# A streaming encoder step on one core: smaller bias write, one mask product a bank, state products and norm moved

## The chip, the core and the metric

The kernel runs on one core of one Trainium2 chip. It uses all engines of that core: TensorE (PE in the rows) for matrix products and transposes into the eight banks of PSUM, VectorE (DVE), ScalarE (ACT), GpSimd (POOL), and the transfer queues that SP, ACT and POOL issue. The metric is device time of one execution in microseconds. The kernel before took 1349.67 us, the median of three runs (1347.54 to 1352.28).

## What is computed

One step of a one-layer encoder over 384 tokens in three tiles of 128: tile 2 is the next 16 frames of eight running streams (the "sample"), tiles 0 and 1 are the 256 frames of a new prompt. Everything is 32-bit float. In short:

```
xn  = rmsnorm(x, g_mix)
q,k,v,o,i,f | aq,ak,av,iq,ik,iw = split(xn @ w_in)
h_m = mLSTM over 4 heads of 128 (with state C, n, m per stream), then headnorm * g_hn * sigmoid(o)
h_a = attention, 8 heads of 64, over the top-k keys that an indexer picks, plus a relative-position bias
h   = x + concat(h_m, h_a) @ w_out
hn  = rmsnorm(h, g_ffn)
s   = (hn @ w_pq) . subkeys            # 8 heads x 2 halves x 128 subkeys
top 16 of each half -> 256 sums -> top 16 -> 16 experts a head, gates = softmax(top 16)
a   = gelu(hn . U[expert])             # 128 experts a token, from a table of 16384
y   = rmsnorm(h + sum(gates * a * V[expert]), g_fin)
```

Outputs are y, the new keys, values and indexer keys, and the new mLSTM states.

## The kernel before

There is one program per engine, written out by hand, with semaphores between them. Two orders rule all. The first is PSUM: a written-out plan (`psum_plan`, L63, and `unit_banks`, L106) names every use of a bank in order; use n takes bank n mod 6, TensorE begins it (`begin`, L878) only when use n - 6 has been read, and either VectorE or ScalarE is its reader. Banks 6 and 7 hold long sums. The second is each engine's own instruction order: a waiting instruction holds all behind it.

**Preparation, streams first.** SP (L409 on) loads inputs and weight chunks of 2 MB into a ring of three (`load_ring`), a step ahead of use. TensorE makes the sample's features chunk by chunk (`sample_features`, L905, and `by_token`, L912). The relative-position bias is one product of a 32-row table (`bvec`, 8 heads x 511 distances, L950). SP writes it to a DRAM scratch once for each of 128 rows (L442), so that a skewed read of the scratch gives every query row its own shift; eight small copies (L448) read the sample's bias back, and LP[0] and LP[1], the prompt's biases, are read by one transfer each (L480, L495). The indexer's scores (L923, name `ri`) lead to the top 36 keys and a mask `negS` of 0 or -1e30 for each token row (L1493). The masked logits `lg` (L986 to L989) are three banks of three, three and two streams; for each stream one product of a 128x128 table `spread` with `negS` adds the mask (L921), then four products of 32 rows add the logits (L923). The spread table is loaded by SP (L445) behind the bias write and the load of the states `CT` (L443).

Then come softmax, attention, mLSTM numerators (L1046), head norm and the output projection of the sample into banks 6 and 7 (L1060 for the attention half, L1069 for the mLSTM half). VectorE adds x (L1611), sums squares (L1399), ScalarE takes the root (L622), VectorE scales by 1/root and g_ffn into `hn` (L1606), TensorE turns `hn` (L1087), ScalarE copies it out (`turned`, L671), and the first query `qs0` starts (`sample_query`, L1101). POOL multiplies the new states' weighted values (L562) and decays the states (L566); `new_state` adds TensorE's product on VectorE (L1622). Scores (L1113) go to VectorE, which picks subkeys and experts (`route_subkeys`, `route_pairs`, `route_experts`, L1632 to L1692). When the first 16 experts a token are known, POOL starts to gather (L580).

**The expert loop.** For each of the three tiles (order 2, 0, 1), 128 gathers bring one expert row pair (U and V, 8 KB) for each of the 128 tokens, 1 MB in all, into one of eight slots. A unit is two experts. VectorE forms the dots (`dots`, L1707), ScalarE gelu, gate and a diagonal (L698 to L707), TensorE adds diag x V to banks 6 and 7 by four matmul records an expert (`weigh`, L1134); a slot is free when that is done. In the first tile every fourth expert (e % 4 == 3) is weighed on VectorE instead (L1717). Into the 64 units of the first tile the whole prompt work is laid, a step a unit (`first_tile`, one function for each engine: L722, L1215, L1780): queries, states, indexer, attention, mLSTM, output projection (L1192), norm, prompt queries (L1145), with weight chunks in two buffers of 2 MB (`load_late`). The later tiles have routing only.

The lines that set what the change touches:

```
L59    return n == 0 and e % 4 == 3                                   # on_vector
L442   sp.dma_start(d["scratch"][:, :, 0:511], over(bvec, 1, P)).then_inc(bvec_out, 16)
L921   mm(o, spread[:, s, :], negS, start=True, stop=False, skip_group_check=True)
L1571  link(v.tensor_tensor(st[:, c:c + 2], st[:, c:c + 2], cols[:, 1, t, 2 * i:2 * i + 2], ALU.max))
L1606  v.scalar_tensor_tensor(hn[t], xr[:, t, :], st[:, lo + 8:lo + 9], gffn, ALU.mult, ALU.mult).then_inc(hn_ok, 1)
L1116  new_state(0); turn_hn(SAMPLE, 1); sample_query(0); new_state(1); scores(0); sample_query(1)   # TensorE, waits left out
L1694  new_state(0); new_state(1); route_subkeys(0, 0); route_pairs(0, 0); route_experts(0)          # VectorE
```

## Time and profile before

| | before |
|---|---|
| median of the runs, us | 1349.67 |
| the profiled execution: its own time / its span, us | 1350.36 / 1348.20 |
| busy: PE, DVE, ACT, POOL, us | 1076.6, 838.3, 391.8, 436.1 |
| mean granted PE clock | 0.937 |
| moved by the transfers | 484.22 MB, 359 GB/s over the span |
| of that, the gathers | 402.68 MB |
| first gather issued; first dots of tile 1; of tile 2, us | 209.9; 670.6; 1024.7 |

The span runs from the first to the last instruction; the execution's own time has 2.16 us around it. Busy shares are means over parts with different limits, so the table is to be read with the windows by stage below. A matmul in 32-bit float is two records in the trace, and their ends are modelled. The granted clock is a share of 2.4 GHz; it has two levels, 1.0 and 0.5.

### The profile page before, as it was taken

The page shows a single profiled execution, that of the slowest core. Times are in us where ns is not written, and L with a number is a line of the kernel's source. Part 1 is how long each engine was busy: PE and PEld are TensorE (multiplying, and loading weights), DVE is VectorE, ACT ScalarE, POOL GpSimd, SP SyncE. Part 2 cuts the span into 40 slices and gives each one's busy share as a digit, 9 for nine tenths or more (in the row PEclk, how much of TensorE's full clock was granted, in tenths as well). Part 3 has the DMA queues.
Part 4 walks back from the last instruction along what each step waited for, and adds up shares of the span by engine and source line. Part 5 has one row for each costly group of instructions (what it writes and reads, how often), then busy time and mean ns, then how long its engine had stood idle before and what let it go on. Part 6 is the DMA issues. An engine that isn't in the chain of part 4 may idle for free.

```text
span 1348.2 us, 11119 instructions
## 1 busy us (share of the span) xinstructions
PE 1076.6 (80%) x3592; PEld 582.9 (43%) x3592; DVE 838.3 (62%) x1949; ACT 391.8 (29%) x1175; POOL 436.1 (32%) x406
## 2 busy tenths in 40 slices
PE   6829975889989999978799877777676777777776
PEld 5719554655635744435465433323222222222222
DVE  3402236769997576766868799996445545454444
ACT  0202002223344344233423333333223222222222
POOL 1000133323332333323333444344343333343431
PEclk9958977989999999989899989889998999999999
DMA  9767409999999989998989999999999999999996
GB/s 359 204 173 272 189 0 375 423 419 363 401 397 367 370 355 423 348 367 339 389 331 344 336 367 395 395 394 409 421 422 381 424 421 421 422 421 422 421 422 264
DMA packets 72520, 484.22 MB, mean 359 GB/s; under 512 B 7464, under 2 KB 17292, under 8 KB 19216
## 3 DMA queue, kind: packets, MB, share of 16 engines
q0 software_dynamic: 55296, 402.68, 74.0%
q1 hardware_dynamic: 16336, 80.08, 16.1%
q10 hardware_dynamic: 832, 0.77, 0.2%
q8 instruction: 28, 0.46, 0.1%
q14 instruction: 28, 0.23, 0.0%
HBM read 475.79 MB, written 7.71 MB: 359 GB/s over the span
## 4 chain that ended last, share of the span: by engine, by line
PE 39%; DMA 27%; DVE 27%; ACT 4%; issue 2%; POOL 0%; DVEq 0%; ACTq 0%; POOLq 0%
DMA arena<-in_peer_uv,arena 23%; PE ps L1134 18%; DVE arena L1707 11%; PE ps L1145 5%; PE ps L912 4%; DMA arena<-in_spreads 3%; PE ps L905 3%; PE ps L1192 2%; ACT arena L701 1%; DVE arena L1635 1%; DVE arena L1642 1%; ACT arena L707 1%; DVE arena L1636 1%; DVE arena L1684 1%; DVE arena L1682 1%
## 5 line engine op out<-in xcount | busy, mean ns | idle before, releaser
L1134 PE MATMUL ps<-arena 128*128 128x512 f32 x1408 | 677.1, 626 | 209.9 <-ACT arena L707 208.3
L580 POOL DMA_INDIRECT arena<-in_peer_uv,arena x384 | 412.3, 1074 | 708.4 <-PE ps L1134 629.4
L1707 DVE CUSTOM_DVE_ANT_0 arena<-arena 128x1024 f32<-128x1024 f32 x380 | 456.5, 1224 | 233.7 <-DMA arena<-in_peer_uv,arena 230.8
L1134 PEld LDWEIGHTS ps<-arena 128*128 128x128 f32 x1408 | 267.4, 198 | 577.4 <-issue 289.5
L698 ACT ACTIVATE arena<-arena 128x2 f32<-128x2 f32 (+1 forms) x194 | 39.4, 203 | 601.4 <-DVE arena L1707 591.9
L1145 PE MATMUL ps<-arena 128*128 128x256 f32 x576 | 131.4, 381 | 0.7 <-ACT arena L607 0.7
L707 ACT ACTIVATE arena<-arena 128x128 f32<-128x128 f32 x352 | 124.0, 395 | 6.3
L1145 PEld LDWEIGHTS ps<-arena 128*128 128x128 f32 x576 | 110.3, 192 | 31.7 <-issue 17.3
L607 ACT ACTIVATE arena<-ps 128x256 f32<-128x256 f32 (+2 forms) x85 | 39.2, 479 | 253.9 <-PE ps L1145 85.3
L701 ACT ACTIVATE arena<-arena 128x1 f32<-128x1 f32 x384 | 92.3, 287 | 6.4
L912 PE MATMUL ps<-arena 128*128 128x512 f32 x144 | 66.0, 613 | 0.0
L562 POOL TENSOR_TENSOR arena<-arena 128x1032 f32<-128x1032 f32 x4 | 8.7, 2178 | 130.9 <-PE ps L1046 107.6
L912 PEld LDWEIGHTS ps<-arena 128*128 128x128 f32 x144 | 28.1, 197 | 34.7 <-issue 34.7
L1717 DVE SCALAR_TENSOR_TENSOR arena<-arena 128x1024 f32<-128x1024 f32 x31 | 39.7, 1280 | 4.0 <-ACT arena L701 4.0
L905 PE MATMUL ps<-arena 128*128 128x128 f32 x320 | 40.8, 293 | 0.8 <-DVE arena L1418 0.8
L905 PEld LDWEIGHTS ps<-arena 128*128 128x128 f32 x320 | 40.1, 209 | 2.5 <-DVE arena L1418 1.2
L1101 PEld LDWEIGHTS ps<-arena 128*128 128x128 f32 x256 | 31.7, 204 | 3.0 <-issue 1.9
L1101 PE MATMUL ps<-arena 128*128 128x128 f32 x256 | 32.1, 288 | 0.7 <-ACT arena L607 0.7
L1707 DVE DVE_READ_ACCUMULATOR2_ANT arena<- 128x1 f32 x380 | 31.0, 82 | 0.0
L698 ACT ACT_TABLE_LOAD x24 | 30.8, 1283 | 0.4
L921 PE MATMUL ps<-arena 128*128 128x144 f32 x16 | 6.8, 526 | 29.6 <-DMA arena<-in_spreads 29.6
L1192 PE MATMUL ps<-arena 128*128 128x512 f32 x64 | 28.8, 592 | 0.0
(223 smaller groups left out, 692.8 us busy)
## 6 DMA issues: line engine op xcount, KB each, us to landing
arena<-in_w_in SPq DMA_DIRECT2D x16, 2048.0 KB, 11.3
arena<-in_w_pq SPq DMA_DIRECT2D x8, 2048.0 KB, 12.5
arena<-in_w_out SPq DMA_DIRECT2D x4, 2048.0 KB, 9.2
arena<-in_peer_uv,arena POOLq DMA_INDIRECT x384
arena<-in_state_C SPq DMA_DIRECT2D x1, 2064.0 KB, 49.4
out_new_C_s<-arena SPq DMA_DIRECT2D x1, 2064.0 KB, 11.9
arena<-in_cache_k SPq DMA_DIRECT2D x4, 512.0 KB, 12.1
arena<-in_cache_v SPq DMA_DIRECT2D x1, 2048.0 KB, 8.8
```

Source lines behind the costliest of these rows:

```text
L580: nc.gpsimd.indirect_dma_start(slots[e % SLOTS], None, d["peer_uv"], bass.IndirectOffsetOnAxis(ap=eidx[:, t, e:e + 1], axis=0)).then_inc(l ...
L698: link(act.activation(gslot[:, k:k + e1 - e0], aslot[:, k:k + e1 - e0], ACT.Gelu_apprx_tanh))
L701: last = act.activation(wslot[:, k:k + 1], gslot[:, k:k + 1], ACT.Copy, scale=gates[:, t, e:e + 1])
L707: act.activation(diag[:, k, :], ident, ACT.Copy, scale=wslot[:, k:k + 1]).then_inc(diag_ok, 1)
L905: last = mm(b[:, P * g:P * g + P], w[:, k, P * g:P * g + P], xn[:, SAMPLE, k, :], start=k == 0, stop=k == KC - 1)
L912: last = mm(b, xn[:, t, k, :], w[:, k, :], start=k == 0, stop=k == KC - 1)
L1101: last = mm(b[:, P * c:P * c + P], w[:, k, P * g:P * g + P], xn[:, SAMPLE, k, :], start=k == 0, stop=k == KC - 1)
L1134: last = mm(ps[:, BANKS + half, :], diag[:, k, :], slots[k][:, DM + 512 * half:DM + 512 * half + 512], start=e == 0, stop=e == HK - 1 or ( ...
L1145: last = mm(b[:, 0:PROMPT], w[:, k, P * f:P * f + P], xp[:, :, k, :], start=k == 0, stop=k == KC - 1)
L1192: last = mm(b, src[:, c, :], w[:, c + 4 if name == "ya" else c, :], start=c == 0, stop=c == 3)
L1707: last = v.tensor_tensor_reduce(slots[k][:, 0:DM], slots[k][:, 0:DM], hn[t], 1.0, 0.0, ALU.mult, ALU.add, aslot[:, k:k + 1])
L1717: link_used(v.scalar_tensor_tensor(acc, slots[k][:, DM:2 * DM], wslot[:, k:k + 1], acc, ALU.mult, ALU.add), n, e)
```

## The change

The scratch holds 16 copies of the bias vector, not 128, and each of the two prompt bias reads becomes 16 copies of 16 partitions. The mask comes by one product a bank: a selector `tsel` of token rows against `negX`, the mask laid out by stream on VectorE. The state's load goes behind two weight loads, the cached keys behind one. POOL's products are gone: ScalarE forms the weighted values by eight scalings a head, and VectorE decays and adds in one instruction a stream. h itself is turned, before its root: the gain g_ffn, turned by TensorE at the start, is applied where the turned h is copied out, and 1/root enters only the exponent of the gates and `hn`. The products of the new states go behind the first scores on TensorE and behind the first routing on VectorE. Nine more experts of the first tile are weighed on VectorE. The products by token of the first tile are cut in two halves a unit apart, and around units 40 to 53 the steps are reordered. The constants' first transfer is split from the gain's.

```diff
 def on_vector(n, e):
-    return n == 0 and e % 4 == 3
+    return n == 0 and (e % 4 == 3 or e % 4 == 1 and 54 <= e < 92)
...
-    add("V", "CN00", "CN01", "CN02")
-    add("A", "hnT20", "hnT21", "qs0")
-    add("V", "CN10", "CN11", "CN12", "sc0")
+    add("V", "hnT20", "hnT21")
+    add("A", "qs0")
+    add("V", "sc0", "CN00", "CN01", "CN02", "CN10", "CN11", "CN12")
...
+            def load_bias(q):
+                for i in range(P // LS):
+                    src = bass.AP(d["scratch"].tensor, 127 + P * (1 - q) - LS * i,
+                                  [[511, LS], [512 * P, HA], [1, P * (q + 1)]])
+                    sp.dma_start(LP[q][LS * i:LS * i + LS], src).then_inc(tb_in[q], 16)
...
+            filled(sp, "iqS")
+            load_ring("av", 0)
             for j in range(JP):
                 sp.dma_start(KT[:, j, :, 0:PAST], d["cache_k"][:, j]).then_inc(cache_in, 16)
-            filled(sp, "iqS")
-            load_ring("av", 0)
...
-            sp.dma_start(d["scratch"][:, :, 0:511], over(bvec, 1, P)).then_inc(bvec_out, 16)
-            sp.dma_start(CT, d["state_C"]).then_inc(state_in, 16)
-            filled(sp, "ri2")
-            sp.dma_start(at(TMP, 1024), d["spreads"][:, 1024:2048]).then_inc(spread_in, 16)
+            sp.dma_start(d["scratch"][:, 0:LS, 0:511], over(bvec, 1, LS)).then_inc(bvec_out, 16)
...
             load_ring("mv", 0)
+            sp.dma_start(CT, d["state_C"]).then_inc(state_in, 16)
...
-            sp.dma_start(LP[0], bass.AP(d["scratch"].tensor, 127 + P, [[511, P], [512 * P, HA], [1, P]])).then_inc(tb_in[0], 16)
+            load_bias(0)
...
-                nc.gpsimd.tensor_tensor(vw[h % 2], over(mv1_2[:, h, :], 1, NB), over(wkm[:, h, :], 2, DX),
-                                        ALU.mult).then_inc(vw_ok, 1)
...
-                nc.gpsimd.tensor_tensor(CT[:, h], CT[:, h], over(decb[:, h, :], 2, DX), ALU.mult).then_inc(ct_ok, 1)
...
+            def weighted_values(h):
...
+                for k in range(NB):
+                    last = act.activation(vw[h % 2][:, k, :], mv1_2[:, h, :], ACT.Copy, scale=wkm[:, h, k:k + 1])
+                last.then_inc(vw_ok, 1)
...
-                    evac(f"hnT{t}{i}", xn[:, t, 4 * i:4 * i + 4, :], bank(f"hnT{t}{i}").rearrange("p (c t) -> p c t", c=4))
+                    for c in range(4):
+                        k = 4 * i + c
+                        last = act.activation(xn[:, t, k, :], bank(f"hnT{t}{i}")[:, P * c:P * c + P], ACT.Copy,
+                                              scale=gffnT[:, k:k + 1])
...
-                act.activation(g, g, ACT.Exp).then_inc(gate_ex, 1)
+                act.activation(g, g, ACT.Exp, scale=rstd[:, t:t + 1]).then_inc(gate_ex, 1)
...
-                elif g == 51:
-                    root(7, 0, 1)
                 elif g == 52:
-                    root(8, 1, 1)
                     turned(0)
                 elif g == 53:
+                    root(7, 0, 1)
+                    root(8, 1, 1)
                     turned(1)
...
+                    if mask is not None:
+                        mm(b[:, 0:n * LK], tsel, mask[:, 3 * i:3 * i + n, :], start=True, stop=False, skip_group_check=True)
...
-                        if add_mask:
-                            mm(o, spread[:, s, :], negS, start=True, stop=False, skip_group_check=True)
...
-            last.then_inc(y2_ok, 1)
+                last.then_inc(y2_ok, 1)
...
-                        last = turn(b[:, P * c:P * c + P], hn[t][:, P * k:P * k + P], ident)
+                        last = turn(b[:, P * c:P * c + P], xr[:, t, P * k:P * k + P], ident)
...
-            new_state(0)
-            turn_hn(SAMPLE, 1)
+            turn_h(SAMPLE)
             was_read(pe, "hnT21")
             sample_query(0)
+            scores(0)
+            new_state(0)
             new_state(1)
-            scores(0)
             sample_query(1)
...
-                elif g == 41:
-                    late_weights("mo")
-                    by_token("moB0", 0, late("mo")[0])
-                    prompt_numerators(0)
+                elif g in (40, 41):
+                    by_token("moB0", 0, late_weights("mo"), (lower, upper)[g - 40])
+                elif g in (42, 43):
+                    if g == 42:
+                        prompt_numerators(0)
+                    by_token("moB1", 1, late_weights("mo"), (lower, upper)[g - 42])
...
                 elif g == 51:
                     project_out("ym", 1, 1)
+                    turn_h(0)
                 elif g == 52:
-                    turn_hn(0, 2)
+                    turn_h(1)
                 elif g == 53:
-                    turn_hn(1, 3)
                     was_read(pe, "hnT11")
                     prompt_feature("qq", 0, "pq0'")
...
-            mask_taken(negS, workS).then_inc(negs_ok, 1)
+            link(mask_taken(negS, workS))
+            v.tensor_tensor(negX, over(negS, 1, NB), over(blk, 2, LK), ALU.mult).then_inc(negs_ok, 1)
...
+                    for k in range(m):
+                        c = CT[:, h, 3 * i + k, :]
+                        ins = v.scalar_tensor_tensor(c, c, decb[:, h, 3 * i + k:3 * i + k + 1], b[:, k, :], ALU.mult, ALU.add)
...
-            new_state(0)
-            new_state(1)
             dve.wait_ge(skv_out, 32)
             route_subkeys(0, 0)
             route_pairs(0, 0)
             route_experts(0)
+            new_state(0)
+            new_state(1)
...
-                    filled(dve, "ym11")
+                    add_mix("ym", 0, 1)
+                elif g == 52:
+                    add_mix("ym", 1, 1)
                     norm_sums(7, 0, 0)
-                elif g == 52:
-                    norm_scale(7, 0, 0)
-                    add_mix("ym", 1, 1)
                     norm_sums(8, 1, 1)
                 elif g == 53:
+                    norm_scale(7, 0, 0)
                     norm_scale(8, 1, 1)
```

## Rows read from the trace of the kernel before

**Rows 1.** Timeline of POOL: start us, us, engine, line, operation, tiles, count, [idle before].

```profile
162.01 1.91 POOL L562 TENSOR_TENSOR arena<-arena 128x1032 f32<-128x1032 f32 x1 [107.63 <-PE ps L1046]
...
209.88 1.15 POOL L580 DMA_INDIRECT arena<-in_peer_uv,arena  x1 [6.98 <-DVE arena L1688]
```

**Rows 2.** Timeline of PE, 34 to 126 us, same columns.

```profile
41.87 3.63 PE L923 MATMUL ps<-arena 128*32 128x144 f32 x64
...
54.80 7.03 PE L912 MATMUL ps<-arena 128*128 128x512 f32 x16
...
93.88 0.82 PE L921 MATMUL ps<-arena 128*128 128x144 f32 x2 [29.61 <-DMA arena<-in_spreads]
...
105.18 8.38 PE L905 MATMUL ps<-arena 128*128 128x128 f32 x64
```

**Rows 3.** Timeline of the transfer queue SP, same columns.

```profile
42.10 0.86 SPq L442 DMA_DIRECT2D scratch<-arena  x1
...
52.16 10.20 SPq L445 DMA_DIRECT2D arena<-in_spreads  x1
87.38 3.58 SPq L448 DMA_DIRECT2D arena<-scratch  x8
...
203.08 0.33 SPq L423 DMA_DIRECT2D arena<-in_w_pq  x1
```

**Rows 4.** Timeline of PE, 170 to 205 us, same columns.

```profile
171.91 0.92 PE L1064 MATMUL ps<-arena 128*128 128x128 f32 x4 [3.21 <-DVE arena L1585]
...
173.52 9.80 PE L1069 MATMUL ps<-arena 128*128 128x512 f32 x16 [0.69 <-ACT arena L607]
...
191.17 6.12 PE L1101 MATMUL ps<-arena 128*128 128x128 f32 x32 [0.69 <-ACT arena L607]
...
197.12 1.91 PE L1079 MATMUL ps<-arena 128*128 128x387 f32 x6
...
199.31 3.74 PE L1101 MATMUL ps<-arena 128*128 128x128 f32 x32
```

**Rows 5.** Windows: busy us of each engine, granted PE clock, DMA share, GB/s.

```profile
209.90:272.20 62.30, 41.60 (x207) 27.85 (x205) 42.54 (x126) 15.73 (x45) 24.28 (x22) 0.88 1.01 415
272.20:400.60 128.40, 115.33 (x392) 70.37 (x392) 112.90 (x262) 41.22 (x124) 40.29 (x36) 0.94 0.99 400
400.60:540.00 139.40, 134.91 (x480) 77.88 (x481) 92.53 (x200) 57.59 (x150) 46.12 (x42) 0.98 0.94 374
540.00:670.60 130.60, 108.93 (x334) 60.38 (x332) 90.72 (x194) 44.88 (x120) 44.47 (x38) 0.95 0.94 362
...
189.20:197.30 8.10, 7.41 (x40) 7.01 (x39) 0.81 (x3) 1.19 (x2) 1.31 (x1) 0.58 0.01 2
...
199.30:203.10 3.80, 3.75 (x34) 3.56 (x32) 3.55 (x18) 0.01 (x1) 3.61 (x2) 1.00 0.00 0
```

**Rows 6.** DMA issues by line: queue, count, KB each, median us to landing.

```profile
arena<-scratch SPq DMA_DIRECT2D x8, 9.0 KB, 3.8
```

**Rows 7.** Timeline of DVE, 117 to 171 us, columns as in Rows 1.

```profile
117.64 1.36 DVE L1538 TENSOR_TENSOR arena<-arena 128x1152 f32<-128x1152 f32 x1
...
168.97 2.07 DVE L1584 TENSOR_TENSOR arena<-arena 128x512 f32<-128x512 f32 x1
```

**Rows 8.** Source line L1571: count, ns min/median/max, first and last start.

```profile
L1571 DVE TENSOR_TENSOR arena<-arena x6: 160/160/1685, 151.4 to 532.7; 128x2 f32<-128x2 f32 x6
```

**Rows 9.** Source line L1717, the weighing on VectorE, same columns.

```profile
L1717 DVE SCALAR_TENSOR_TENSOR arena<-arena x31: 1275/1280/1286, 247.9 to 659.0; 128x1024 f32<-128x1024 f32 x31
```

**Rows 10.** Timeline of PE, 577 to 607 us, columns as in Rows 1.

```profile
577.56 1.88 PE L1134 MATMUL ps<-arena 128*128 128x512 f32 x4
...
587.96 5.66 PE L1134 MATMUL ps<-arena 128*128 128x512 f32 x8 [5.09 <-ACT arena L707]
...
597.70 2.77 PE L1134 MATMUL ps<-arena 128*128 128x512 f32 x4 [3.20 <-ACT arena L707]
...
602.86 3.72 PE L1145 MATMUL ps<-arena 128*128 128x256 f32 x16 [0.69 <-ACT arena L607]
```

More of the change, by code:

```diff
@@ L907, in sample_features, with by_token, per_stream @@
                 end(last)
-            def by_token(name, t, w):
-                b = begin(name)
-                for k in range(KC):
+            def by_token(name, t, w, ks=range(KC)):
+                b = begin(name) if ks[0] == 0 else bank(name)
+                for k in ks:
                     last = mm(b, xn[:, t, k, :], w[:, k, :], start=k == 0, stop=k == KC - 1)
-                end(last)
-            def per_stream(name, lhs, rhs_of, add_mask):
+                if ks[-1] == KC - 1:
+                    end(last)
+            lower, upper = range(KC // 2), range(KC // 2, KC)
+            def per_stream(name, lhs, rhs_of, mask):
                 for i in range(3):
                     b = begin(f"{name}{i}")
-                    for s in range(3 * i, min(NB, 3 * i + 3)):
+                    n = min(3, NB - 3 * i)
+                    if mask is not None:
+                        mm(b[:, 0:n * LK], tsel, mask[:, 3 * i:3 * i + n, :], start=True, stop=False, skip_group_check=True)
+                    for s in range(3 * i, 3 * i + n):
                         o = b[:, LK * (s - 3 * i):LK * (s - 3 * i) + LK]
-                        if add_mask:
-                            mm(o, spread[:, s, :], negS, start=True, stop=False, skip_group_check=True)
                         for j in range(JP):
                             last = mm(o[32 * j:32 * j + 32, :], lhs[:, j, s].rearrange("p a t -> p (a t)"), rhs_of(j, s),
-                                      start=not add_mask, stop=True, skip_group_check=True)
+                                      start=mask is None, stop=True, skip_group_check=True)
                     end(last)
-            pe.wait_ge(con_in, 32)
+            pe.wait_ge(con_in, 16)
             turn_x(SAMPLE, 1)
@@ L950, in _ @@
             end(mm(b[0:HA, 0:511], relb, onehot, start=True, stop=True))
+            b = begin("gfT")
+            pe.wait_ge(gfft_in, 16)
+            end(turn(b[:, 0:KC], gfrow, ident[0:KC, 0:KC]))
             b = begin("wht")
@@ L1245, in first_tile @@
                     logits("lp11", "lp12", "lp13")
[L1246 to L1251 removed]
+                elif 23 <= g <= 26:
+                    by_token(f"avB{(g - 23) // 2}", (g - 23) // 2, late_weights("av"), (lower, upper)[(g - 23) % 2])
+                    if g == 26:
+                        scores(4)
                 elif 27 <= g <= 30:
```

165 lines of the change are left out of this document (85 added, 80 removed), and 10 rows, old and new, of the table first.

## The prediction

> **What bounds the kernel now.** I read POOL's first gather first, to part the program in two, then TensorE's idle time and the transfer queue's issues ahead of it, and last the loop's windows. Up to the first gather, issued at 209.88 us [rows 1], the program prepares the streams' tile on one long dependent chain. After it come 384 gathers of 1 MB, eight ahead, in three tiles of 64 units.
>
> In the preparation one wait stands out: TensorE sits idle for 29.6 us before the masked logits, released by a transfer out of the spread table [rows 2]. The queue shows why. The bias vector's write to the scratch is issued at 42.1; the spread table, second behind it, takes 10.2 us to issue at all; and the copies that wait for the write are issued at 87.4 [rows 3]. So the write takes 45.3 us for 1,024 rows of 2 KB, and the table is stuck behind it. The later part of that chain, from 161 on, is paced by VectorE beside POOL's products [rows 1], by TensorE at its lower clock, and by the norm between the output projection and the first query [rows 4].
>
> In the first tile the bound changes hands. From 209.9 to 272.2 the transfers are full: 415 GB/s, busy share 1.01; from there to 400.6 still 400 GB/s. From 400.6 to 540.0 TensorE is busy 134.9 of 139.4 us, while VectorE has 92.5 and transfers run at 374 GB/s [rows 5]: TensorE decides. From 540.0 to 670.6 TensorE has holes again. The second and third tile stay as they are: the change touches nothing there.
>
> **The change, part by part.** Times are against the profiled execution (1350.36 us, of which 1348.20 are span); the median of the runs is 0.69 lower, which I take off at the end.
>
> *Bias write and mask.* The write falls from 128 to 16 copies of the vector. 45.3 us by an eighth is 5.7; it lands near 50, and the eight copies that wait for it, 3.6 us of issue and 3.8 to land [rows 3, 6], are in by 60. The spread table is gone, so TensorE goes on where it became idle, at 93.88 - 29.61 = 64.3 [rows 2]. What is late next: VectorE must first widen the mask to eight streams, one instruction of the size of the softmax scaling, 1.36 us [rows 7]. TensorE works on other products until 64.3 in any case, so that is covered; without the cover it would cost those 1.4. The token selector, the turned gain's transpose and its two small copies I put at 0.4 on the way: **-29.2**, ends -29.6 and -28.8.
>
> The masked logits took from 93.88 to 105.18, 11.3 us. The products alone run in 3.63, as the indexer's do (same count and shape). A mask product over 432 columns costs two records of 0.44 x 432/512 = 0.37 us (0.44 from sixteen records in 7.03), the three together 2.0 [rows 2]. 11.3 - 5.6 = **-5.7**; at the lower clock -3. The next feature product took 8.38 for 64 records, where 32 of that shape take 3.74 [rows 2, 4]: **-0.9**, ends -0.9 and 0.
>
> The state's load moves behind two weight loads and the cached keys behind one, each 5 us at 415 GB/s. The keys are read after the indexer's products, past 45.5 [rows 2], the state only after two feature products and the whole attention. I count nothing for both; without that cover they would cost 10 and 5.
>
> *From the numerators to the first query.* POOL's state products go, half to ScalarE (sixteen small scalings while TensorE runs the output projection; POOL did eight in 1.91 [rows 1]) and half into VectorE's state sum. Beside POOL's products one of six two-element VectorE products took 1.685 us, where the median is 0.160 [rows 8], and a 512-element one 2.07 where 1.36 x 512/1152 = 0.6 would do [rows 7]. These two give 2.9 of the 3.2 us that TensorE idles before turning the heads [rows 4]: **-2.9**. The projection after it took 9.80 for sixteen records that run in 7.03 elsewhere, the first query 6.12 where the second took 3.74 [rows 2, 4]; the granted clock was 0.58 around the first query and 1.00 around the second [rows 5], that is mostly 1.2 GHz against 2.4. Without the holes ahead of them I expect the higher level: **-2.8** and **-2.4**, or 0 and 0 if the clock falls anyway. From the end of the projection (183.3) to the first query (191.2) pass 7.9 us of adding, squares, root, scaling, turning and copying. With h turned at once only the second half's add, its turn and its copy are left, about 0.6 + 0.5 + 0.6 and the gaps between, 2.3: **-5.6**. Last, the second head's state products (1.9 us on TensorE, of which I count 1.3 ahead of the scores) go behind the scores [rows 4]: **-1.3**. Sum of this stage **-15.0**, ends -15.6 and -9.8. Up to the first gather that makes -50.8: it starts near 159.
>
> *After the first gather.* All six state banks now wait for VectorE until the routing is over, and the second query needs one of them. It ended at 203.05, 6.8 us before the first gather [rows 1, 4]; now it ends about 7 behind it. The 2 MB load that waits for it left at 203.08 [rows 3] and moved ahead of the gathers; now it moves among them. At 415 GB/s that is 5.1 us; from 272 to 400 the transfers have 4% left and may take up some of it: **+4**, ends 0 and +5.
>
> The prompt biases come as 32 copies in place of two, each issued in 0.45 us [rows 3], so SP is held twice for some 7 us. The weight load behind the first set goes out near 15 us after the first gather; its reader on TensorE stands behind six experts and two queries, so I count nothing, and 7 if that cover is gone. The rows show the eight small copies overlapping: one leaves every 0.45 us and takes 3.8 to land [rows 3, 6]. The Trainium skill says otherwise of such sizes ("DMA: Bandwidth & Descriptors", section Bandwidth): batch transfers to 1 MiB, those under 64 KB are descriptor-dominated; its fit has about 2.0 us fixed for each. One after another by that figure, an estimate, sixteen copies take some 35 us, and the second set would reach its reader some 3 us late; by the rows it is in time.
>
> *Nine more experts on VectorE.* Experts 57, 61 to 89 leave TensorE in units 28 to 44. One costs TensorE four records of 0.44 us [rows 2], nine 15.8. VectorE takes nine times 1.28 = 11.5 [rows 9] and has 47 us free in that window. The transfers set a floor: 374 GB/s x 139.4 us at 415 GB/s are 125.6 [rows 5], so 13.8 can go. I take **-12**, ends -15.8 and -6. The halved feature products only spread TensorE's work: 0.
>
> *Norm of the prompt.* From unit 51's products to the first prompt query pass 602.86 - 577.56 = 25.3 us; 9.0 are waits (5.09, 3.20, 0.69), and part of the work ran slow behind them [rows 10]. With h turned at once the work is about 12 us. New waits come: the next dots on VectorE stand behind two sums of squares, and ScalarE does two roots and eight scalings before the first prompt query may start. I put them at 5: 25.3 - 17 = 8.3, taken as **-7.5**, ends -9 and -3.
>
> Sum: -29.2 - 5.7 - 0.9 - 15.0 + 4 - 12 - 7.5 = -66.3. 1350.36 - 66.3 = 1284.1, less 0.7 is **1283.4 us**. All good ends give 1273, all bad ends 1304.
>
> **Rivals.** *The transfers hold the loop.* They already run at 362 to 400 GB/s from 272 on [rows 5], and the weight loads come in pairs. If the gathers behind them set the pace, the two gains in the loop (19.5) vanish: 1302.9. For it: the share near 1. Against it: the 374 GB/s where TensorE is full. Chance 0.15.
>
> *The write stays long.* If it is not the number of rows that costs but something else on the way of this write, the copies still leave at 87.4 and the last lands at 94.8; the first bank of logits, full at about 98.1 before, is then read 3.3 us earlier and not 29.2: 1309. Against it: nothing but rows fills those 45.3 us. Chance 0.04.
>
> *VectorE in lockstep, slower than before.* An expert weighed on VectorE stands behind ScalarE's weight for it and ahead of the next dots. So far every second unit from 27 to 46 has one; with the change nearly every unit does. If each of the nine new ones cost VectorE its lead, a whole unit of 139.4/19 = 7.3 us, and its own 1.28 lay on the path, 9 x 8.6 = 77 us would come on top: 1361. It decides from 7.4 us for each. Against it: the longest of TensorE's waits for ScalarE in the rows is 5.09 [rows 10], and eight gathers lie ahead. Chance 0.04.
>
> **How the numbers follow.** The forecast has 0.77, with 1283.4 as its value. The range 1270 to 1305 takes in its ends, a little beyond the good one for the clock, and the first rival; the other two and the tails are left out, under 2 in 10. A measurement of this kernel can tell about 0.3%, 4 us, from no change. Faster: 0.77 + 0.15 + 0.04 = 0.96; the lockstep rival gives 0.03 to slower and 0.01 to the break-even.
>
> **What would show it.** Right: TensorE's masked logits begin near 64 and end near 70; the first gather is issued between 156 and 164; from unit 27 to 46 TensorE's busy time falls by some 15 us; the first prompt query follows unit 51's products by about 17 us; the last two tiles take 677 us as before. Wrong: a new wait of TensorE behind the scratch copies, the projection still at 9.8 us, or VectorE idle ahead of its weighing (now line 1717) by more than a few microseconds in all.

## The result and the profile after

The changed kernel takes 1286.97 us, the median of four runs (1283.15 to 1292.07), against 1350.66 before in four runs: a ratio of 0.953, 95% interval 0.949 to 0.957. The forecast was 1283.4, range 1270 to 1305. The profiled execution took 1292.07 us, the longest of the four, where that of before took 1350.36: 58.3 us less, by which the terms below are measured.

The first gather in the timeline of GpSimd, then TensorE's masked logits, then the transfer queue around the write to the scratch (start us, us, engine, line, operation, tiles, count, [idle before]):

```profile
158.12 1.11 POOL L574 DMA_INDIRECT arena<-in_peer_uv,arena  x1 [102.99 <-DVE arena L1722]
```

```profile
64.95 0.99 PE L940 MATMUL ps<-arena 128*128 128x432 f32 x2
65.87 0.94 PE L944 MATMUL ps<-arena 128*32 128x144 f32 x24
...
69.85 7.41 PE L921 MATMUL ps<-arena 128*128 128x128 f32 x64
```

```profile
43.00 0.34 SPq L454 DMA_DIRECT2D scratch<-arena  x1
50.50 3.57 SPq L457 DMA_DIRECT2D arena<-scratch  x8
```

The gather stood at 209.88 [rows 1], the masked logits at 93.88 behind 29.61 us of idle time, the next feature product at 105.18 [rows 2]. The copies that wait for the write now leave 7.5 us after it, where it was 45.3 [rows 3], and no idle time stands ahead of the logits.

TensorE from the last transposes of the heads to the second query, to set beside [rows 4]:

```profile
132.23 0.60 PE L1088 MATMUL ps<-arena 128*128 128x128 f32 x4
133.52 7.13 PE L1093 MATMUL ps<-arena 128*128 128x512 f32 x16 [0.69 <-ACT arena L601]
140.49 0.60 PE L1112 MATMUL ps<-arena 128*128 128x128 f32 x4
...
142.94 3.84 PE L1126 MATMUL ps<-arena 128*128 128x128 f32 x32 [0.78 <-DVE arena L1641]
...
159.28 5.70 PE L1126 MATMUL ps<-arena 128*128 128x128 f32 x32 [7.55 <-DVE arena L1657]
```

The projection takes 7.13 us and the first query 3.84 (9.80 and 6.12 before). The second query now ends 6.9 us behind the first gather.

The loop, by windows as in [rows 5]: from the first gather to unit 27, to 46, to 64:

```profile
158.10:363.70 205.60, 172.12 (x692) 113.13 (x692) 161.85 (x414) 62.99 (x191) 65.29 (x60) 0.91 1.00 382
363.70:491.50 127.80, 118.59 (x441) 70.05 (x441) 103.69 (x208) 54.62 (x138) 44.01 (x41) 0.97 0.98 402
491.50:611.90 120.40, 104.42 (x329) 58.20 (x327) 90.91 (x194) 44.93 (x131) 45.19 (x38) 0.97 1.00 406
```

The same three stretches took 190.7, 139.4 and 130.6 us before, at 405, 374 and 362 GB/s. So the first lost 14.9 us, the others gained 11.6 and 10.2. What is new in the first are two waits for transfers, one of TensorE and one of VectorE (waits from 158 to 400; none of the kind stood there before):

```profile
PE ps L1126 <- DMA arena<-in_w_pq: 13.5, 1, 13.5
```

```profile
DVE arena L1793 <- DMA arena<-scratch: 6.6, 1, 6.6
```

TensorE's is for the third query load, which stands behind the eight copies of tile 0's prompt bias; VectorE's is for the eight copies of tile 1's (each prompt bias comes by eight copies, not by the 16 that the section on the change and the prediction have). On the transfer queue:

```profile
165.14 0.33 SPq L428 DMA_DIRECT2D arena<-in_w_pq  x1
165.51 6.31 SPq L435 DMA_DIRECT2D arena<-scratch  x8
173.49 1.80 SPq L428 DMA_DIRECT2D arena<-in_w_pq  x1
...
301.80 5.20 SPq L435 DMA_DIRECT2D arena<-scratch  x8
```

### The profile page after: what moved, and what is told of

Its sections match the earlier page's. It is cut to its first block, busy times and chain, and to the rows that moved or that the text cites. A ratio compares the mean times of both kernels' runs of the same rounds, so it can differ in the third digit from the quotient of the medians.

```text
span 1290.3 us, 11110 instructions
## 1 busy us (share of the span) xinstructions
PE 1051.2 (81%) x3547; PEld 571.2 (44%) x3547; DVE 850.6 (66%) x1983; ACT 398.5 (31%) x1207; POOL 420.9 (33%) x398
## 4 chain that ended last, share of the span: by engine, by line
PE 39%; DMA 28%; DVE 26%; ACT 4%; issue 3%; SPq 0%; POOL 0%; DVEq 0%; ACTq 0%; POOLq 0%
DMA arena<-in_peer_uv,arena 21%; PE ps L1159 18%; DVE arena L1741 11%; PE ps L1170 5%; PE ps L929 4%; PE ps L921 3%; DMA arena<-scratch 3%; DMA arena<-in_w_pq 3%; PE ps L1126 2%; PE ps L1217 2%; DVE arena L1669 1%; DVE arena L1676 1%; ACT arena L715 1%; DVE arena L1670 1%; ACT arena L721 1%
## 5 line engine op out<-in xcount | busy, mean ns | idle before, releaser
L1159 PE MATMUL ps<-arena 128*128 128x512 f32 x1372 | 659.4, 625 | 189.0 <-ACT arena L721 185.5
L1159 PEld LDWEIGHTS ps<-arena 128*128 128x128 f32 x1372 | 260.0, 198 | 547.1 <-ACT arena L721 276.7
L1170 PEld LDWEIGHTS ps<-arena 128*128 128x128 f32 x576 | 110.6, 192 | 33.8 <-issue 17.8
L721 ACT ACTIVATE arena<-arena 128x128 f32<-128x128 f32 x343 | 121.4, 395 | 6.4
L601 ACT ACTIVATE arena<-ps 128x256 f32<-128x256 f32 (+2 forms) x79 | 35.7, 468 | 213.8 <-PE ps L1170 77.9
L929 PE MATMUL ps<-arena 128*128 128x512 f32 x144 | 67.1, 614 | 0.0
L1751 DVE SCALAR_TENSOR_TENSOR arena<-arena 128x1024 f32<-128x1024 f32 x40 | 51.3, 1282 | 1.0 <-ACT arena L715 1.0
L1126 PE MATMUL ps<-arena 128*128 128x128 f32 x256 | 33.6, 296 | 21.9 <-DMA arena<-in_w_pq 13.5
L1126 PEld LDWEIGHTS ps<-arena 128*128 128x128 f32 x256 | 32.9, 211 | 24.7 <-issue 15.8
L929 PEld LDWEIGHTS ps<-arena 128*128 128x128 f32 x144 | 28.1, 198 | 33.7 <-issue 33.7
L921 PEld LDWEIGHTS ps<-arena 128*128 128x128 f32 x320 | 38.6, 202 | 2.2 <-DVE arena L1440 1.2
L1217 PE MATMUL ps<-arena 128*128 128x512 f32 x64 | 28.8, 592 | 0.0
L1676 DVE FIND_INDEX8 arena<-arena 128x8 uint32<-128x128 f32 (+1 forms) x72 | 23.2, 330 | 0.0
L1666 DVE MAX8 arena<-ps 128x8 f32<-128x128 f32 x24 | 7.1, 296 | 20.6 <-PE ps L1138 20.5
```

The source lines that it names most:

```text
L721: act.activation(diag[:, k, :], ident, ACT.Copy, scale=wslot[:, k:k + 1]).then_inc(diag_ok, 1)
L921: last = mm(b[:, P * g:P * g + P], w[:, k, P * g:P * g + P], xn[:, SAMPLE, k, :], start=k == 0, stop=k == KC - 1)
L929: last = mm(b, xn[:, t, k, :], w[:, k, :], start=k == 0, stop=k == KC - 1)
L1126: last = mm(b[:, P * c:P * c + P], w[:, k, P * g:P * g + P], xn[:, SAMPLE, k, :], start=k == 0, stop=k == KC - 1)
L1159: last = mm(ps[:, BANKS + half, :], diag[:, k, :], slots[k][:, DM + 512 * half:DM + 512 * half + 512], start=e == 0, stop=e == HK - 1 or ( ...
L1170: last = mm(b[:, 0:PROMPT], w[:, k, P * f:P * f + P], xp[:, :, k, :], start=k == 0, stop=k == KC - 1)
```

## The experiments

Each kernel is the changed one but for its edit, timed against the kernel before. The question is where 14.9 us went behind the first gather. Theory A: late landings hold the engines, and each wait is the price. Theory B: the transfers are full there, and bytes (and what they move at) are the price, whatever waits.

One thing must be known first. The changed kernel and the four of the first and fifth experiment run the same instructions on TensorE, VectorE and ScalarE up to the first gather, and yet it comes at 158.1, 153.9, 154.1, 157.9 and 152.2 us in their profiles. Of the 6.0 us between the first and the last of them, 1.0 stands by 88 us, 2.3 come in the products just ahead of one projection, and 2.7 over its own 16 records, here in these two:

```profile
99.65 9.86 PE L929 MATMUL ps<-arena 128*128 128x512 f32 x16
```

```profile
96.44 7.11 PE L929 MATMUL ps<-arena 128*128 128x512 f32 x16
```

The granted clock over them was 0.72 in the one and 1.00 in the other, and 0.50 (1.2 GHz) just ahead of the slow one, though TensorE had not stood idle there. So this part comes and goes between executions of the same code, and what an edit does behind the first gather is counted from the first gather ("the stretch" below is from there to unit 27). This count has a spread too: the changed kernel and the runs of the fifth and sixth experiment, whose code is the same in that stretch, took 205.6, 204.4 and 203.2 us over it.

**Order of the prompt-bias copies.** Tile 0's copies ahead of the second query load; tile 1's ahead of a 2 MB weight load; both.

```diff
-            filled(sp, "qs1")
-            load_late("pq2")
             filled(sp, "hnT21")
             load_bias(0)
+            filled(sp, "qs1")
+            load_late("pq2")
...
-            filled(sp, "aqB3")
-            load_late("av")
             sp.wait_ge(relu_used, 6)
             sp.wait_ge(state_out, 16)
             load_bias(1)
+            filled(sp, "aqB3")
+            load_late("av")
```

> Against the changed kernel (1287.0 median; profiled 1292.07). The copies of tile 0's prompt bias are issued right after the heads' last bank is turned, near 141, and so ahead of the first gather at 158; the second 2 MB query load still waits for the second query and leaves near 165, the third near 167 to 173. Theory A (late landings hold the engines): the third load lands by 195, TensorE's wait for it falls from 13.5 us to under 2, unit 8 starts 8 to 11 us earlier than the 233.1 of the changed kernel, and 5 to 7 us of that are still there at unit 20 and at the end: 1280 to 1282. Theory B (the transfers are full and only bytes count, the wait lies beside a backlog of gathers): the wait goes too and unit 8 starts earlier, but at units 12 to 20 only the 0.5 MB that moved ahead of the gathers is left, 1.3 us at 415 GB/s, and so at the end: 1285 to 1287.

Measured: 1279.49 us (1275.55 to 1284.65; ratio to before 0.948, 0.946 to 0.950), 7.5 below the changed kernel. TensorE's wait for the third load is gone. From the first gather to unit 27 it takes 200.0 us, 5.6 less.

> The eight copies of tile 1's prompt bias leave one weight load earlier, near 282 instead of 301.8, as soon as the buffers are free. Theory A: they still take 35 to 40 us to land, but by 322, ahead of their reader near 338, so VectorE's 6.6 us wait for them goes, unit 27 starts 6 to 8 us earlier than 363.7 and the end too: 1279 to 1281. Theory B: the wait goes, but the weight load behind them or the gathers come later by as much, unit 27 moves by less than 2 us and the end by less than 2: 1285 to 1287.

Measured: 1287.49 us (0.955, 0.953 to 0.957), no change. VectorE's wait is gone, yet the stretch takes 205.9 us (205.6).

> Both orders at once. Theory A for both: 11 to 15 us, 1272 to 1276. B for the first and A for the second: 7 to 9 us, 1278 to 1280. B for both: 1 to 2 us, 1285 to 1286.

Measured: 1283.90 us (0.950, 0.949 to 0.952); the stretch takes 198.3 us, 1.7 less than with the first edit alone, which is within that spread, and at the end, counted from the first gather, the two are 0.3 apart.

This fits none of its three forecasts. What follows: a wait that goes need not give time. Removing TensorE's 13.5 us gave 5.6, removing VectorE's 6.6 gave nothing. The stretch is full of transfers (busy share 1.00), so what counts is bytes and rate. The next two groups look at the rate.

**Rows written.** 64 and 128 rows, with two copies and one copy for each prompt bias (here 128; the step and the count of the wait follow).

```diff
-            sp.dma_start(d["scratch"][:, 0:LS, 0:511], over(bvec, 1, LS)).then_inc(bvec_out, 16)
+            sp.dma_start(d["scratch"][:, 0:128, 0:511], over(bvec, 1, 128)).then_inc(bvec_out, 16)
```

> 64 rows, two copies for each prompt bias. By rows the write takes 24 us, the sample's bias is in near 75, and VectorE reads the masked logits some 6 to 8 us later than in the changed kernel: first gather 6 to 8 us later, 1293 to 1295 with the waits after it as they are. Theory copies: TensorE's wait for the third query load under 6 us and 4 us less. Theory packets: over 10 us.

> The changed kernel with the bias vector written to all 128 rows again, and one copy for each prompt bias in place of eight; no spread table comes back. By rows (0.34 us a row and 2.1 fixed, from 7.5 us for 16 and 45.3 for 128) the write lands near 88, the sample's bias near 96; TensorE's masked logits still begin near 65, but VectorE can read them only from 96 on and the first gather is 26 to 29 us later than in the changed kernel. If the write's time hung on the spread table behind it, it would land near 50 and the first gather would stay within 2 us. After the first gather: if it is the number of copies that made the prompt biases slow, the single copy behind the second query load lands within 10 us, TensorE's wait for the third query load (13.5 us) falls under 4, and 5 us come back; if it is their 1,024 small packets among the gathers, the wait stays over 10 us. Total 1308 to 1316.

Measured: 1295.27 us (0.958, 0.955 to 0.961) and 1306.66 (0.969, 0.966 to 0.972). The transfer queue of the two:

```profile
42.92 0.34 SPq L454 DMA_DIRECT2D scratch<-arena  x1
66.25 3.57 SPq L457 DMA_DIRECT2D arena<-scratch  x8
```

```profile
43.60 0.86 SPq L454 DMA_DIRECT2D scratch<-arena  x1
88.50 3.58 SPq L457 DMA_DIRECT2D arena<-scratch  x8
```

16, 64 and 128 rows hold the queue for 7.5, 23.3 and 44.9 us: straight in the rows, 0.33 us each. With 128 VectorE waits 29.1 us for the sample's bias and the first gather is 29.6 later; with 64 it waits 7.5, and the first gather is 10.6 later (TensorE runs at a granted clock of 0.50 from 93.5 to 110.6, behind its own hole). Behind the first gather both give time back: the stretch to unit 27 takes 196.1 and 191.0 us, and TensorE still waits 10.1 and 10.4 for the third load. So neither theory held as put: the wait stays, as the theory of packets has it, and the time returns, as the theory of copies has it (with 128 rows the total is also 1.3 below its forecast). The transfers while tile 0's rows pass, in the changed kernel (176 to 202.5) and with 128 rows (206.7 to 227.6); q0 are the gathers, q1 the copies and loads:

```profile
DMA packets 2326, 9.28 MB, mean 350 GB/s; under 512 B 255, under 2 KB 1275, under 8 KB 1275
## 3 DMA queue, kind: packets, MB, share of 16 engines
q0 software_dynamic: 1161, 8.46, 91.3%
q1 hardware_dynamic: 1164, 0.80, 11.0%
```

```profile
DMA packets 2118, 8.67 MB, mean 415 GB/s; under 512 B 130, under 2 KB 1151, under 8 KB 1151
## 3 DMA queue, kind: packets, MB, share of 16 engines
q0 software_dynamic: 1053, 7.70, 89.2%
q1 hardware_dynamic: 1064, 0.95, 13.4%
```

Two things are to be seen. In both, the two queues' packets pass in equal numbers: a 512 byte packet gets one turn for each packet of the gathers, so 1,024 of them last as long as some 1,000 gather packets, over 20 us, where ahead of the gathers they take 4 (138.9 to 142.8 in the first experiment). And beside the eight narrow copies a gather packet takes longer: 91.3% of 16 engines over 26.5 us for 1161 packets are 0.333 us each, against 0.283 with one wide copy (the 8 KB ones alone, 1033 in 8.46 MB, 0.373 and 0.316), and the transfers move 350 GB/s in place of 415. While tile 1's rows of 1 KB pass (311 to 343.7 in the changed kernel) it is 315:

```profile
DMA packets 2382, 10.29 MB, mean 315 GB/s; under 512 B 265, under 2 KB 1287, under 8 KB 1287
## 3 DMA queue, kind: packets, MB, share of 16 engines
q0 software_dynamic: 1189, 8.69, 85.5%
q1 hardware_dynamic: 1191, 1.57, 16.9%
```

By an estimate from these rows, 26.5 us at 350 and 32.7 us at 315 in place of 415 cost 4.2 and 7.9 us, some 12 in all. Without the first 4.2, and without the 0.5 MB themselves (1.3 us), 5.5 us should come back, and with tile 0's copies ahead of the gathers 5.6 did.

**Which partitions a copy writes.** Eight copies as before; in the first kernel each to every eighth partition, in the second each brings one head to all 128 (24 rows written).

```diff
-                    src = bass.AP(d["scratch"].tensor, 127 + P * (1 - q) - LS * i,
-                                  [[511, LS], [512 * P, HA], [1, P * (q + 1)]])
-                    sp.dma_start(LP[q][LS * i:LS * i + LS], src).then_inc(tb_in[q], 16)
+                    src = bass.AP(d["scratch"].tensor, 127 + P * (1 - q) - i,
+                                  [[512 - P // LS, LS], [512 * P, HA], [1, P * (q + 1)]])
+                    sp.dma_start(LP[q][i:P:P // LS], src).then_inc(tb_in[q], 16)
```

> The changed kernel, its write of 16 rows as it is, and each of the eight copies still writes 16 partitions, but every eighth one of the 128 and not 16 neighbours. Theory count: as the changed kernel, 1285 to 1289. Theory neighbours (partitions lying together share a way in, spread ones share less): the 8 KB packets beside the copies take 0.32 to 0.34 us, unit 12 starts 3 to 5 us earlier counted from the first gather and unit 27 some 8 to 10: 1277 to 1281. If only the number of partitions that one copy writes counts, wherever they lie: as the changed kernel.

Measured: 1279.71 us (0.949, 0.947 to 0.952), 7.3 below the changed kernel; the stretch takes 195.9 us, 9.7 less. While tile 0's rows pass (172.5 to 197):

```profile
DMA packets 2371, 9.80 MB, mean 400 GB/s; under 512 B 258, under 2 KB 1278, under 8 KB 1278
## 3 DMA queue, kind: packets, MB, share of 16 engines
q0 software_dynamic: 1181, 8.63, 88.3%
q1 hardware_dynamic: 1189, 1.16, 14.6%
```

The same copies, bytes and packets, but 400 GB/s and 0.293 us a gather packet (8 KB: 0.328). So it is not the number of copies but that each writes 16 neighbours. (Each copy's rows also start at other columns of the scratch; that this counts was not tried.) VectorE's wait for tile 1's copies falls from 6.6 to 1.5 us, TensorE's stays at 13.9, and the time returns all the same. The Trainium skill ("SBUF — State Buffer", section Door 1: The DMA port swizzle) has a transfer's bandwidth depend on how many of 16 ports its partitions reach; by its table 16 neighbours reach 4, every eighth of 128 reaches 8, all 128 reach 16. That is the rate of a transfer itself. What the traces show is the rate of the gathers beside the copies, and it has the same order (319, 352 and 368 GB/s): the narrow copy slows the packets of others.

```diff
-                for i in range(P // LS):
-                    src = bass.AP(d["scratch"].tensor, 127 + P * (1 - q) - LS * i,
-                                  [[511, LS], [512 * P, HA], [1, P * (q + 1)]])
-                    sp.dma_start(LP[q][LS * i:LS * i + LS], src).then_inc(tb_in[q], 16)
+                for h in range(HA):
+                    src = bass.AP(d["scratch"].tensor, 512 * P * h + 127 + P * (1 - q),
+                                  [[512 - LS, P // LS], [511, LS], [1, P * (q + 1)]])
+                    sp.dma_start(LP[q][:, h], src).then_inc(tb_in[q], 16)
```

> The changed kernel with the prompt biases again in eight copies each, of the same bytes and the same 1,024 rows, but each copy brings one head to all 128 partitions, where the changed kernel brings all heads to 16 partitions (the scratch gets 24 rows for that, the write some 2.7 us more, which nothing waits for). In the runs with fewer copies the gathers' 8 KB packets beside them took 0.337 us (two copies of 64 partitions) and 0.316 (one of 128), in the changed kernel 0.373 (eight of 16). Theory count: it is the number of copies, the packets stay near 0.37, TensorE waits 13 us for the third query load, VectorE 6 us for tile 1's bias, the end stays at 1285 to 1289. Theory partitions: it is how few partitions one copy writes, the packets take 0.32, the rows of tile 0's bias pass in 21 us and not 26.7, and as with one copy unit 12 starts 4 to 6 us earlier counted from the first gather, unit 27 some 10 to 14: 1272 to 1278.

Measured: 1305.31 us (0.966, 0.964 to 0.969), 18 slower than the changed kernel: outside both theories. Its queue:

```profile
165.28 24.34 SPq L435 DMA_DIRECT2D arena<-scratch  x8
189.66 5.13 SPq L428 DMA_DIRECT2D arena<-in_w_pq  x1
...
303.86 26.61 SPq L435 DMA_DIRECT2D arena<-scratch  x8
```

The gather packets did get shorter (8 KB: 0.332), but the issue of eight copies took 24.3 us in place of 6.3, and the rows passed in 34.5. Ahead of the gathers, where nothing else moves, eight such copies (in the run by head of the last experiment) leave 64 packets under 512 bytes (the semaphores), the copies of the first experiment 128:

```profile
DMA packets 1089, 0.54 MB, mean 106 GB/s; under 512 B 64, under 2 KB 1088, under 8 KB 1088
```

```profile
DMA packets 1152, 0.52 MB, mean 125 GB/s; under 512 B 128, under 2 KB 1152, under 8 KB 1152
```

Eight semaphores a copy and not sixteen: the rows went to half of the 16 engines, each then has twice as many turns to wait for. Among the gathers it shows as one packet of the copies for two of the gathers (176 to 196):

```profile
q0 software_dynamic: 1047, 7.64, 96.9%
q1 hardware_dynamic: 502, 0.24, 4.9%
```

The Trainium skill ("DMA: Bandwidth & Descriptors", section Why a DMA increments its semaphore by 16 and not by 1) gives a transfer the largest number of engines up to 16 that divides the slowest dimension on both sides, here 8 and 128, so 8; the count agrees. TensorE then waited 21.8 us for the third load and VectorE 17.1 for tile 1's bias, the busy share of the stretch fell to 0.93, and here the waits did cost.

**The second query ahead of the state products**, with tile 0's copies first (TensorE's part; ScalarE's copy and the order of banks follow).

```diff
             scores(0)
+            sample_query(1)
             new_state(0)
             new_state(1)
-            sample_query(1)
```

> The second head's query goes ahead of the state products again (on TensorE, on ScalarE and in the order of banks), and the copies of tile 0's prompt bias stay ahead of the first gather, as in the run before that did that alone (1279.5 median). The second 2 MB query load then leaves near 151 instead of 161 to 165 and moves ahead of the gathers. Theory B (bytes that move behind the first gather cost their time, 5.1 us at 415 GB/s for 2 MB): units 12 to 27, counted from the first gather, start 4 to 5 us earlier than in that run, and the end too: 1275. Theory A' (the loop has slack for those bytes once no engine waits): under 1.5 us, 1278 to 1280.

Measured: 1274.62 us (0.943, 0.941 to 0.946). The stretch takes 192.8 us, 7.2 less than with the copies alone, at the same rate (391 GB/s, 390 there): the bytes that run in it fell from 78.0 to 75.4 MB. Bytes that move behind the first gather cost their time: 2.6 MB at 390 GB/s are 6.7 us. The median is 4.9 lower.

**The nine experts.**

```diff
-    return n == 0 and (e % 4 == 3 or e % 4 == 1 and 54 <= e < 92)
+    return n == 0 and e % 4 == 3
```

> The nine added experts go back to TensorE, nothing else changes. The forecast's term: 12 us slower (ends 6 and 15.8), 1299, with TensorE busy some 16 us more between units 27 and 46 and the distance of these units at the 139.4 us of before, where the changed kernel has 127.8. Rival, the transfers hold that stretch: under 2 us, 1287 to 1289.

Measured: 1293.60 us (0.959, 0.958 to 0.961), 6.6 slower than the changed kernel. Its units 27 to 46:

```profile
356.60:491.10 134.50, 131.34 (x472) 76.36 (x473) 92.44 (x200) 57.59 (x147) 43.76 (x40) 0.97 0.98 391
```

134.5 us against 127.8 (126.4 to 129.9 in the other kernels that keep the nine): 6.7 for the nine. TensorE's busy time fell by 12.7 with them, but at 402 GB/s and a share of 0.98 the transfers take over. Another 4.9 of the 11.6 us came without them (139.4 to 134.5).

**GpSimd beside VectorE.** The semaphore and a later wait of VectorE for it are left out here.

```diff
+            filled(pool, "NUM21")
+            for k in range(4):
+                nc.gpsimd.tensor_tensor(qbd_f, qbd_f, qbd_f, ALU.mult).then_inc(beside, 1)
+                pool.wait_ge(beside, k + 1)
```

> The changed kernel with four products of 128x1024 put on GpSimd beside VectorE's last sums before the heads are turned, over a buffer that nothing reads any more; nothing else moves. The forecast's price: one two-element product takes 1.7 us in place of 0.16 and 512-element ones 1.7 to 2.1 in place of 0.6 to 0.7, together 2.9 us or a little more, and TensorE idles that long again before turning the heads; the projection behind the idle time falls to the lower clock and takes 9.8 us in place of 7.1, the first query 6.1 in place of 3.8: first gather 3 to 8 us later, 1290 to 1295. Rival: the sums were slow for another reason, first gather within 1 us.

Measured: 1293.56 us (0.958, 0.955 to 0.961). VectorE and then TensorE:

```profile
125.67 1.57 DVE L1604 TENSOR_TENSOR arena<-arena 128x2 f32<-128x2 f32 x1
...
132.36 2.05 DVE L1617 TENSOR_TENSOR arena<-arena 128x512 f32<-128x512 f32 x1
```

```profile
135.28 0.77 PE L1095 MATMUL ps<-arena 128*128 128x128 f32 x4 [3.17 <-DVE arena L1618]
136.74 9.96 PE L1100 MATMUL ps<-arena 128*128 128x512 f32 x16 [0.69 <-ACT arena L608]
...
148.98 3.84 PE L1133 MATMUL ps<-arena 128*128 128x128 f32 x32 [0.79 <-DVE arena L1648]
```

The two products take 1.57 and 2.05 us, without GpSimd 0.16 and 0.69; TensorE idles 3.17 and its projection runs at 0.71 of the clock, 9.96 us. The first gather comes 6.8 us later. The first query, at a distance from the hole, kept its 3.84, where 6.1 was expected.

**Together.** By-head copies, and then spread copies, with the second query and tile 0's copies moved ahead.

> Three parts together: tile 0's prompt bias ahead of the first gather, the second query ahead of the state products, and the copies by head. The first two gave 1274.6. Theory partitions: VectorE's wait for tile 1's bias (about 7 us) goes too: 1266 to 1270. Theory count: 1273 to 1276.

Measured: 1284.57 us (0.953, 0.950 to 0.955). Both of its theories are missed. Tile 1's copies are issued over 26.6 us here too, and VectorE waits 16.9 for them.

> Three parts together: tile 0's prompt bias ahead of the first gather, the second query ahead of the state products (these two gave 1274.6), and each of the eight copies over every eighth partition. Tile 0's copies run before the gathers in any case, so only tile 1's gain: the 8 KB packets beside them take 0.34 us in place of 0.38, VectorE's wait for them (about 7 us) falls under 1, unit 27 starts about 5 us earlier counted from the first gather: 1268 to 1271. If the spread copies gained only where tile 0's bias moved among the gathers: 1274 to 1276.

Measured: 1268.25 us (1267.15 to 1272.93; 0.941, 0.939 to 0.943), 18.7 below the changed kernel, the fastest of all. The stretch takes 186.1 us, less than before the change:

```profile
152.40:338.50 186.10, 166.97 (x660) 107.95 (x660) 161.41 (x414) 62.74 (x189) 70.27 (x60) 0.94 1.00 407
```

VectorE's wait for tile 1's copies is 1.9 us, 6.3 without the spread. But part of the 18.7 lies ahead of the first gather, which came at 152.4 in this execution and at 158.1 in the changed kernel's. From the first gather to the end of the span it takes 1116.7 us, 15.5 less than the changed kernel (1132.2) and only 2.2 less than without the spread (1118.9): of the 6.7 us that the stretch gains by the spread here, units 27 to 64 lose 4.1 (252.0 and 247.9). Why is open. Spread copies alone kept all their gain, 9.6 us at the end.

From the first gather to unit 27, for eight of the kernels (us, GB/s, and their product):

| kernel | us | GB/s | MB |
|---|---|---|---|
| before | 190.7 | 405 | 77.2 |
| changed | 205.6 | 382 | 78.5 |
| tile 1's copies first | 205.9 | 385 | 79.3 |
| tile 0's copies first | 200.0 | 390 | 78.0 |
| spread copies | 195.9 | 400 | 78.4 |
| one copy (128 rows) | 191.0 | 411 | 78.5 |
| tile 0's copies and second query first | 192.8 | 391 | 75.4 |
| the same, spread copies | 186.1 | 407 | 75.7 |

In all of these the busy share is 0.99 or 1.00. The changed kernel's 1.3 MB more make 3 us at 405 GB/s; the other 12 of its 14.9 us are rate, as much as the estimate for the two sets of copies.

## Why the prediction was right, and where not

| term | forecast | ends | measured |
|---|---|---|---|
| masked logits start | -29.2 | -29.6, -28.8 | -28.9 (93.88 to 64.95) |
| masked logits | -5.7 | -5.7, -3 | -6.4 (11.30 to 4.90) |
| next feature product | -0.9 | -0.9, 0 | -1.0 (8.38 to 7.41) |
| heads to first query | -15.0 | -15.6, -9.8 | -15.0 |
| (first gather) | -50.8 | | -51.8 |
| first gather to unit 27 | +4 | 0, +5 | **+14.9** |
| units 27 to 46 | -12 | -15.8, -6 | -11.6, the nine experts 6.7 of it |
| units 46 to 64 | -7.5 | -9, -3 | -10.2 |
| rest | 0 | | +0.4 |

*Write and mask.* Right, and by the reason given: an eighth of 45.3 us (5.7) was forecast, 7.5 came, and the runs with 64 and 128 rows show the price by the row. The rival of a write that stays long is out. The cover of VectorE's widening held, and so did that of the moved loads: up to the first gather TensorE waits for one transfer only, at the start (10.1 us).

*Heads to first query.* Its five parts came at -3.4, -2.7, -5.6, -2.3 and -1.0, against -2.9, -2.8, -5.6, -2.4 and -1.3. That GpSimd slowed VectorE, the run with its products put back shows. In the same run the hole and the slow projection came back together, in one trace; that the clock falls for the hole is not more than that, since at 95 us of the changed kernel it fell with no hole ahead. What the first query gained (2.3) that run leaves open: the query kept its 3.84 there. In the kernel before, TensorE had stood idle for 3.74 us ahead of the turning that feeds it, and no run put that back.

*After the first gather: the step that failed.* One of the signs of being wrong that the prediction names came: a new wait of TensorE behind the scratch copies. The forecast had +4, for 2 MB that move behind the first gather, and counted nothing for the prompt biases, their cover being six experts and two queries for the load behind the first set and a timely landing for the second. The cover was short by 13.5 and 6.6 us of waits. But these waits are not the price either, as the moved and the spread copies show: with transfers full, the price is the rate that eight copies to 16 neighbouring partitions cost the gathers for as long as they take turns with them, some 12 us for both sets, a term that the forecast put at nothing. [Rows 6] showed eight copies overlapping, of 9 KB and with no gathers running; from that row no such price could be read. The forecast also took 32 copies where there are 16. That undoes its working of the other way: with a fixed 2.0 us for each of sixteen copies, the second set was to come some 3 us late, but with eight that is about half of the 35 us, an estimate, and the set is in time. It came 6.6 late; spread over the partitions the same eight copies are 1.5 late, and ahead of the gathers all eight of a set take 4 us: a fixed time for each is not what held them. The fixed 2.0 us is a fit of the Trainium skill ("DMA: Bandwidth & Descriptors", section Anatomy of one DMA — SWDGE (gpsimd) path), for transfers that GpSimd issues, where these are issued by SP; and the rule that the prediction quotes from that page, for transfers under 64 KB, does not reach copies of 64 and 128 KB.

*Nine experts.* The term's size fits, by luck, and its cause only by half: 6.7 us are theirs, near the weak end of 6, since the transfers take over where TensorE leaves off. So the first rival, that the transfers hold the loop, was partly true of this term, and not of the norm. Where the other 4.9 come from was not tried; TensorE is busy 3.6 us less in these units even without the nine, so some of its work lies earlier than before.

*Norm.* From unit 51's products (527.02) to the first prompt query (543.10) pass 16.1 us, where 25.3 stood before and 17 was forecast. The whole term, units 46 to 64, came 1.2 us beyond its good end. No run undid this part alone, so its cause is argued from the forecast and not shown.

*Lockstep.* VectorE stood idle ahead of its weighing for 1.0 us in all: out.

*The number.* It is nearer than the mechanism deserves. The profiled execution stands 8.0 us above the forecast's sum: +10.9 behind the first gather, +0.4 in the experts' term and +0.4 in the rest, against -1.0 ahead of the first gather and -2.7 in the norm. The median is 3.6 above the forecast, since that execution lies 5.1 above its median, with the clock's fall in its preparation; that the other three had less of it is likely by the profiles of the same code, but they have no trace. So that the median lies 3.6 us off, with one term off by 10.9, is in part luck.

## What to carry to other kernels

Where the transfers are full, don't price a small transfer by its bytes or by the wait behind it: count its packets, each of which takes a turn beside a large one, and look at how many partitions it writes, because a narrow one slows its neighbours too. Put such transfers ahead of the full stretch, or spread each over the partitions. As long as the transfers' busy share stays at 1.00, a wait in the profile is a sign of late transfers and not the price (by head it fell to 0.93, and the waits cost): take the wait away and see whether the stretch gets shorter, counted from an event that both kernels share.

## What the runs showed of the hardware that was not expected

- Packets of two queues took turns one by one (1161 to 1164, 1181 to 1189, 1053 to 1064), though one's were of 8 KB and most of the other's of 512 bytes; with one queue on half of the engines, two for one (1047 to 502).
- Copies to 16 neighbouring partitions stretched the gathers' 8 KB packets beside them from 0.316 us (one copy to 128 partitions) to 0.373; to 16 spread partitions 0.328.
- A copy whose pattern's slowest dimension was 8 left 8 semaphore packets and not 16, and eight of them among gathers held the queue 24.3 us in place of 6.3.
- The same code ran one projection in 7.11 us at a granted clock of 1.00 and in 9.86 at 0.72, a large part of what set the first gather between 152.2 and 158.1 us.
